# Coarser operand waits on TensorE and two reordered VectorE steps at four hand-overs of a two-block kernel

## The reference, cut to what matters

```python
# per group g of 8: y = scan output * silu(z), then
yg = yg * lax.rsqrt(jnp.mean(yg * yg, axis=-1, keepdims=True) + EPS)
y = (yg.reshape(bsz, seqlen, D_SSM) * ssm_norm_w)
p_ssm = y @ w_ssm_out
y_conv = cb * causal_depthwise_conv(cc * cx, conv_w)
p_conv = y_conv @ w_conv_out
g_conv, g_ssm = jnp.split(jax.nn.sigmoid(gl), 2, axis=-1)
merged = g_conv * p_conv + g_ssm * p_ssm
x = x + gate1 * (merged @ w_o)
u2 = rms_norm(x, ln2[i]) * (1.0 + scale2) + shift2
hid = jnp.square(jax.nn.relu(u2 @ w_up[i]))
x = x + gate2 * (hid @ w_down[i])
```

## Time and profile before

| | |
|---|---|
| median of 3 executions | 2321.96 us (2321.91 to 2323.67) |
| the profiled execution | 2321.96 us, its span 2320.2 us |
| TensorE busy | 2250.2 us, 97% of the span |
| VectorE busy | 1321.6 us, 57% |
| ScalarE busy | 859.7 us, 37% |
| mean granted TensorE clock | 0.986 |

### The profile page before, as it was taken

How to read it: one execution, slowest core, us unless ns; L and a number is a source line. 1 busy time by engine, 2 the same in 40 slices (tenths; PEclk the granted TensorE clock), 3 DMA queues, 4 the chain that set the end, 5 groups by cost and what they waited for, 6 DMA issues and landing times.

```text
span 2320.2 us, 28538 instructions
## 1 busy us (share of the span) xinstructions
PE 2250.2 (97%) x10868; PEld 1837.4 (79%) x10868; DVE 1321.6 (57%) x1837; ACT 859.7 (37%) x1219; POOL 5.4 (0%) x8
## 2 busy tenths in 40 slices
PE   7999999999999999999999999999989899999998
PEld 4777777787888898888878888889868667888887
DVE  5567777777674375433476344355777655434344
ACT  5555555542222242322342222234454444222224
POOL 0000000000000000000000000000000000000000
PEclk8999999999999999999999999999999799999999
DMA  6322222224452334232222322223120002222321
GB/s 245 109 91 91 90 90 90 90 73 145 164 181 91 107 111 128 91 104 94 90 91 91 102 92 97 91 88 93 49 68 33 19 19 88 94 91 91 104 87 64
DMA packets 207100, 222.08 MB, mean 96 GB/s; under 512 B 9397, under 2 KB 199290, under 8 KB 204954
## 3 DMA queue, kind: packets, MB, share of 16 engines
q1 hardware_dynamic: 205322, 210.26, 28.4%
q10 hardware_dynamic: 1680, 10.49, 1.1%
HBM read 218.57 MB, written 2.16 MB: 95 GB/s over the span
## 4 chain that ended last, share of the span: by engine, by line
PE 80%; DVE 8%; ACT 6%; issue 5%; DMA 1%; ACTq 0%; DVEq 0%; POOL 0%; SPq 0%; POOLq 0%
PE G L547 22%; PE G L549 22%; PE G L548 22%; PE G L583 2%; PE G L585 2%; PE G L584 2%; ACT whi L1153 1%; DVE wlo L1769 1%; PE G L1020 1%; PE X L735 1%; PE X L1037 1%; ACT seg L1284 1%; DVE rinv L1819 1%; PE X L1003 1%; PE X L1027 1%
## 5 line engine op out<-in xcount | busy, mean ns | idle before, releaser
L547 PE MATMUL G<-ahi,whi 128*128 128x512 f32 x1496 | 603.5, 403 | 8.1 <-DVE wlo L1769 4.0
L548 PE MATMUL G<-alo,whi 128*128 128x512 f32 x1496 | 592.7, 396 | 0.0
L549 PE MATMUL G<-ahi,wlo 128*128 128x512 f32 x1496 | 592.6, 396 | 0.0
L1769 DVE TENSOR_TENSOR wlo<-raw,whi 128x2048 fp32r<-128x2048 f32 x177 | 405.7, 2292 | 295.8 <-ACT whi L1153 292.6
L1153 ACT ACTIVATE whi<-raw 128x2048 fp32r<-128x2048 f32 x177 | 337.4, 1906 | 351.4 <-PE G L549 315.3
L547 PEld LDWEIGHTS G<-ahi,whi 128*128 128x128 f32 x1496 | 283.3, 189 | 76.5 <-DVE wlo L1769 4.2
L548 PEld LDWEIGHTS G<-alo,whi 128*128 128x128 f32 x1496 | 283.3, 189 | 66.9 <-issue 2.2
L549 PEld LDWEIGHTS G<-ahi,wlo 128*128 128x128 f32 x1496 | 282.9, 189 | 67.2
L547 PE MATMUL G<-hhi,whi 128*128 128x512 f32 x784 | 310.1, 396 | 0.1
L548 PE MATMUL G<-hlo,whi 128*128 128x512 f32 x784 | 309.4, 395 | 0.0
L549 PE MATMUL G<-hhi,wlo 128*128 128x512 f32 x784 | 309.4, 395 | 0.0
(11 more groups left out here) (401 smaller groups left out, 2800.3 us busy)
## 6 DMA issues: line engine op xcount, KB each, us to landing
raw<-in_w_in SPq DMA_DIRECT2D x44, 1024.0 KB, 5.3
raw<-in_w_up SPq DMA_DIRECT2D x38, 1024.0 KB, 5.4
raw<-in_w_down SPq DMA_DIRECT2D x32, 1024.0 KB, 5.1
raw<-in_w_gate SPq DMA_DIRECT2D x22, 1024.0 KB, 5.3
braw<-in_w_ada SPq DMA_DIRECT2D x12, 1024.0 KB, 5.1
raw<-in_w_in SPq DMA_DIRECT2D x18, 512.0 KB, 5.1
araw<-in_w_ada ACTq DMA_DIRECT2D x8, 1024.0 KB, 18.0
bc<-acum_dram SPq DMA_DIRECT2D x8, 1024.0 KB, 6.0
```

The costliest lines, as they stand in the source:

```text
L547: pe.matmul(bank[:], wh[:, j, f], rh[:, j, :], start=(j == 0), stop=False)
L548: pe.matmul(bank[:], wh[:, j, f], rl[:, j, :], start=False, stop=False)
L549: last = pe.matmul(bank[:], wl[:, j, f], rh[:, j, :], start=False, stop=(j == k - 1))
L1769: tt(wlo[s][:], raw[s][:], r32(whi[s][:]), ALU.subtract).then_inc(lo_split, 1)
```

## The change

On TensorE three waits for operands become coarser: the output unit of the last group waits for both blocks of `ylo` at its start; the wait for `blo` stands ahead of the loop of four turns, so that it lies ahead of the first gate unit, which does not read `blo`; the first `w_o` unit waits for all 8 blocks of `clo` at its start. On VectorE, `unit()` (the low part of the unit after the last group's output unit) moves behind `add_group`, and the wait for `ada_used` with its addition moves ahead of the `unit()` that makes the low part of the second `w_down` unit. Nothing is computed otherwise than before.

```diff
@@ TensorE, last group's output unit
             s = next_unit()
+            operand(2)
             for m in range(KB):
-                fm_tile(s, m, yhi, ylo, k=2, n=D, b=(2 * s + m) % 4, each=None if m else t["op"])
-            t["op"].add(2)
+                fm_tile(s, m, yhi, ylo, k=2, n=D, b=(2 * s + m) % 4)
@@ TensorE, gate and w_conv units, then w_o
-            t["op"].add(KB)
+            operand(KB)
             with turns(pe, 4, t, both):
                 fm_unit(ahi, alo)
-                pe.wait_ge(act_ready, t["op"].now())
                 fm_unit(bhi, blo)
+            operand(KB)
             for u in range(2):
-                fm_unit(chi, clo, each=None if u else t["op"])
-            t["op"].add(KB)
+                fm_unit(chi, clo)
@@ VectorE, last group's output unit
             taps = conv_taps(1)
-            s = unit()
-            add_group(s, lambda m: next(taps, None))
+            add_group(slot[0] ^ 1, lambda m: next(taps, None))
+            unit()
@@ VectorE, feed-forward part
+                if first:
+                    dve.wait_ge(ada_used, 24)
+                    link(tt(modT[:, 5, :], X[3][:, 40:48], badaT[:, 40:48], ALU.add))
+                    dve.sem_inc(x_free[3], 1)
                 for u in range(4):
                     s = unit()
-                    if first and u == 0:
-                        dve.wait_ge(ada_used, 24)
-                        link(tt(modT[:, 5, :], X[3][:, 40:48], badaT[:, 40:48], ALU.add))
-                        dve.sem_inc(x_free[3], 1)
```

## The result

| | before | after |
|---|---|---|
| median | 2321.96 us (2320.56 to 2323.67, 5 runs) | 2338.83 us (2334.29 to 2343.06, 5 runs) |
| ratio | | 1.0076, 95% interval 1.0064 to 1.0087 |
| profiled execution | 2321.96 us, span 2320.2 | 2338.22 us, span 2336.4 |
| forecast | | 2338.0 us, range 2332.5 to 2342.0 |

The account below looks back on a forecast made before the run. TensorE, busy 97% of the span, was taken as the bound. Waits of 2.24 + 2.47 + 3.68 + 2.84 = 11.23 us plus 4.8 us for clock falls made 16.0 us over 2321.96: 2338.0 us, range 2332.5 to 2342.0.

Parts of the forecast that it names:

- Place 1: Last group's output unit: coarser `ylo` wait and `unit()` behind `add_group` start the gate unit 2.24 us later.
- Place 2: Ahead of the gate loop: the first gate unit now waits for the last `blo`, +2.47 us.
- Place 3: First `w_o` unit: waiting for all of `clo` removes the cover of 21 matmuls, +3.68 us.
- Place 4: Second `w_down` unit: its low part runs only after the `ada_used` wait and addition, TensorE +2.84 us.
- The waits together: Sum of TensorE's added waits at the four places: 11.23 us.
- The clock: Behind the four new gaps: three falls to half clock, 1.6 us each, 4.8 us in all.
- the prediction's bound: Clock cost of the four new gaps, bounded by gaps in the trace of before: nothing to 6.4 us.
- The prediction's own sign of being wrong: Beyond 1700 us: half-clock time changed by more than some microseconds would make the prediction wrong.
- The rival "not slower": Half-clock stretch from 1808 us goes away, giving "no change" from a gain of 11 us; shifted late stretch 0.07.
- The bound of 13.5 us given back: Late stretch, 1808 to 1836 us: run at full clock it would give back at most half, 13.5 us.
- The argument from three executions within 1.8 us of each other: Whole kernel before: its three executions lie within 1.8 us, held against the late stretch going away.

Follow-up runs that it names:

- move1: Kernel before with only `unit()` moved behind `add_group`, without the coarser wait for `ylo`; the gate unit came 1.67 us later.
- the fillers: Changed kernel plus 3, 2, 3 and 2 idle matmuls with unread results in its four new gaps; 2335.3 us, ratio 1.006 to before.
- the late kernel: Kernel before plus six idle matmuls in TensorE's gaps at 1806 to 1810 and at 1826 us; ratio 0.9991 (0.9979 to 1.0004).

## Why the prediction was right

**Place 1: right.** 2.24 us was forecast, 2.28 measured, by the forecast path: additions keep up, the wait for `pacc` goes, the low part starts 0.6 us behind the last addition. Taken apart, the wait alone was free and the move alone cost 1.67 us, as was expected for the two kernels (0.0 and 1.6).

**Place 2: mechanism right, size short.** 2.47 us was forecast, 2.66 (alone 2.83) measured. The chain of `blo` ended when it was said to, 705.84 + 0.69 = 706.53; but the first matmul came 0.33 us behind it, where the latency taken from `ylo` was 0.14; what made it longer is not shown. The three later turns lost nothing.

**Place 3: mechanism right, size a little long.** 3.68 us forecast, of which 0.1 us was for the slower step from the first matmul to the second. To the first matmul 3.49 us were measured (3.58 forecast), to the second 3.60; the first matmul followed the low part at 0.05 us instead of 0.14. The 21 matmuls that had covered the chain now stand behind it.

**Place 4: right to the hundredth.** 2.84 us forecast and measured. A small wait that was free behind `unit()` costs the whole 2.3 us of `unit()` and more when it stands ahead of it, because it is released only by the work that `unit()` has to be ready behind.

**The waits together:** 11.23 us forecast, 11.27 measured (11.38 with place 3 taken to its second matmul, as the forecast took it). No later wait absorbed any of it: that for `alo` stayed at 1.2 us.

**The clock: mechanism right, the sum in part by luck.** Three falls, 4.8 us, were forecast. In the first profile there were two, 3.3 us. A further 2.5 us came from more half clock behind 1700 us, which no term of the sum had, and the kernel's start was 1.0 us shorter; that the total of the profiled execution met the forecast to 0.2 us is luck to that extent. In the second profile there were three falls, at places 1, 2 and 3, which cost 1.47, 1.50 and 1.71 us, 4.7 together; there the late part cost 4.8 us more than before. Over all profiles with idle gaps (the four kernels of one place, move1, and the changed kernel twice) the clock fell behind 9 of 13 gaps: 2 of 4 at place 1 (3.06 us), 3 of 3 at place 2 (2.5 to 2.7), 3 of 3 at place 3 (3.3), 1 of 3 at place 4 (2.7). That the falls belong to the gaps, the fillers show. But the prediction's bound, which took a gap of 1.98 us as the longest without a fall and one of 1.70 us as the shortest with one, left out the gap of 1.21 us in its own trace, behind which the clock fell too; the number three was a guess between none and four. The Trainium skill ("TensorE: Matmul & The Clock Gate", Part 1) says that the count of slow matmuls differs between runs of one kernel; it was only cited, since no row showed it. By that rule, these traces agree: behind the same gap of 3.06 us at place 1 the changed kernel's clock stayed up in one execution and fell in the next.

**The prediction's own sign of being wrong.** It named a change of the half clock beyond 1700 us by more than some microseconds. By the granted clock in the traces that was 42.7 us before, 47.5 in the first profile of the changed kernel and 56.9 in the second, and TensorE's matmuls behind 910 us came 2.5 and 4.8 us later for it. So this part did move, and in the second profile by more than the sign allows.

**The rival "not slower".** The late stretch stayed, 27 us at half clock in both profiles of the changed kernel. The bound of 13.5 us given back was far too wide: it took TensorE to be the limit in that piece, and with most of it at full clock the late kernel was only 1.8 us shorter there. The argument from three executions within 1.8 us of each other does not hold either: 35 later executions of the kernel before spread from 2316.41 to 2329.88 us.

**Open.** Why a fall lasts 3.4 us in most places and 6.8 us behind place 3 alone, and what decides behind which gap the clock falls. The time behind 910 us varies with the falls there, in kernels that are equal in that part: before has 6.8 us of half clock from 1910.91 on, the changed kernel has none at the matching matmuls in its first profile and gains 2.7 us there, while it loses 2.9 us between 1650 and 1800 us (in the times of before), where it has 10.2 us of half clock against 3.4, and 2.3 us by a stretch from 1874.49 on that before does not have.

## What to carry to other kernels

A wait on an in-order queue costs the work that it puts behind its release, not its own length: ask of each what stands behind it and whether that work was the cover (a gate unit that reads nothing of the operand, 21 matmuls of the same tile, a low part of weights). A coarser wait can be free as long as something else at the same hand-over ends later, and begins to cost when a second edit takes that away, so measure such edits apart as well as together. And where TensorE is the bound, a new idle gap costs more than its length: in this kernel the clock fell behind 9 of 13 gaps of 2.5 to 3.3 us, for a further 1.6 us each in most cases, and a gap of 1.21 us was no protection. Where TensorE waits for other engines anyway, half clock costs little.

## What the runs showed of the hardware that was not expected

- The clock did not fall by the length of the gap: behind 3.06 us it stayed up in two executions and fell in two, behind 2.5 to 2.7 us at place 2 in all three, and behind a gap of 1.21 us in six profiles of thirteen.
- Matmuls with unread results in a gap, 0.9 us each, kept the clock at 1.00 at all four places in the one profile taken, and raised it from 0.57 to 0.92 in the late stretch; there they bought 1.8 us only.
- The time from the end of a low part of an operand to the first matmul that had waited for it was 0.05 (`clo`), 0.10 (`ylo`) and 0.33 us (`blo`) at three places of one execution.
